# Branch A of an attention layer: transposed scores in blocks of 512 queries, row maxima from a product of their own, key tiles added on GpSimd

## What is computed

```python
s = jnp.einsum("btkgd,bskd->bkgts", q, k).astype(jnp.float32) * (q.shape[-1] ** -0.5)
p = jax.nn.softmax(s, axis=-1)
o = jnp.einsum("bkgts,bskd->btkgd", p.astype(v.dtype), v)
```

## Time and profile before

| | us |
|---|---|
| median of 3 runs | 5053.31 (5050.79 to 5055.74) |
| the profiled execution, its own time | 5050.44 |
| its span | 5048.9 |
| TensorE busy | 4546.0, 90% |
| VectorE busy | 3321.3, 66% |
| ScalarE busy | 2466.6, 49% |
| GpSimd busy | 1194.2, 24% |

### The profile page before, as it was taken

How to read it: one execution, slowest core, us unless ns; L and a number is a source line. 1 busy time by engine, 2 the same in 40 slices (tenths; PEclk the granted TensorE clock), 3 DMA queues, 4 the chain that set the end, 5 groups by cost and what they waited for, 6 DMA issues and landing times. The chain is left out here.

```text
span 5048.9 us, 75988 instructions
## 1 busy us (share of the span) xinstructions
PE 4546.0 (90%) x25973; PEld 3779.7 (75%) x25973; DVE 3321.3 (66%) x5284; ACT 2466.6 (49%) x3062; POOL 1194.2 (24%) x921
## 2 busy tenths in 40 slices
...
GB/s 186 204 120 146 63 77 80 96 177 144 206 198 174 192 214 261 397 397 397 397 359 176 190 99 147 63 88 98 124 193 209 120 163 166 384 397 397 397 397 334
DMA packets 580935, 1089.06 MB, mean 216 GB/s; under 512 B 111781, under 2 KB 265541, under 8 KB 577689
## 3 DMA queue, kind: packets, MB, share of 16 engines
...
## 5 line engine op out<-in xcount | busy, mean ns | idle before, releaser
L630 PE MATMUL project_proj_acc<-project_w_split,project_hT 128*128 128x512 f32 x2736 | 657.3, 397 | 4.1 <-DVE project_w_split L453 2.9
L1719 PE MATMUL merge_acc<-ahead_wide,merge_w_split 128*128 128x512 f32 (+1 forms) x2880 | 638.0, 376 | 21.8 <-DMA ahead_wide<-hT 14.4
L1719 PEld LDWEIGHTS merge_acc<-ahead_wide,merge_w_split 128*128 128x128 f32 x2880 | 504.9, 190 | 129.7 <-issue 21.5
L630 PEld LDWEIGHTS project_proj_acc<-project_w_split,project_hT 128*128 128x128 f32 x2736 | 511.5, 190 | 113.6 <-DVE project_hT L483 4.7
L2418 DVE TENSOR_TENSOR experts_w_gate<-experts_raw_gate,experts_w_gate 128x2048 fp32r<-128x2048 f32 x146 | 370.7, 2548 | 286.7 <-ACT experts_w_gate L2314 286.7
L2293 POOL TENSOR_TENSOR experts_w_down<-experts_raw_down,experts_w_down 128x2048 fp32r<-128x2048 f32 x73 | 354.4, 4855 | 512.1 <-ACT experts_w_down L2314 512.1
L947 DVE TENSOR_REDUCE attend_stat<-attend_scores 128x1 f32<-128x1280 f32 (+2 forms) x288 | 305.6, 1061 | 232.7 <-PE attend_scores L848 229.1
L2465 PE MATMUL experts_gate_acc<-experts_w_gate,experts_rowsT 128*128 128x512 f32 x1752 | 433.5, 403 | 12.3 <-DVE experts_rowsT L2423 6.5
L2479 PE MATMUL experts_result_acc<-experts_w_down,experts_hiddenT 128*128 128x512 f32 x1752 | 430.2, 401 | 12.2 <-DVE experts_w_down L2418 12.2
L2465 PE MATMUL experts_up_acc<-experts_w_up,experts_rowsT 128*128 128x512 f32 x1752 | 420.7, 396 | 0.0
L2465 PEld LDWEIGHTS experts_gate_acc<-experts_w_gate,experts_rowsT 128*128 128x128 f32 x1752 | 328.1, 191 | 99.5 <-issue 19.7
...
## 6 DMA issues: line engine op xcount, KB each, us to landing
...
experts_raw_up<-in_w_exp_up_dram SPq DMA_DIRECT2D x146, 1024.0 KB, 12.8
...
attend_keys<-qk SPq DMA_DIRECT2D x128, 320.0 KB, 5.8
...
```

Of the source, the lines that this page charges most:

```text
L630: m = pe.matmul(acc[g % 2][:, :], hT[:, a, q * KP + k, t * P:(t + 1) * P], w_split[:, n % SLOTS, c, k, :], start=(q == 0 and i == 0 and k ...
L1719: m = pe.matmul(acc[:, b, 0:w], w_split[b][:, a, k, :], hT[:, x, k, 0:w], start=(i == 0 and k == 0), stop=(i == 2 and k == KD - 1))
```

## The change

`attend_gqa` is split: branch C keeps it as `attend_c`, and branch A becomes `attend_a`, written out without a loop. Its unit is a span: one head and 512 latent queries (16 spans in a layer), or, in layer 0, the 256 context queries of both heads of a pair (4 spans more, third of the five of each pair). A span goes through its ten key tiles in five slots of two tiles (a context span has one slot).

- Keys are stationary and queries move, so that the scores come out transposed: for each key tile one product with 64 rows of high keys and a row of ones against the high queries and a row that holds the negative row maximum, and one product for the low parts; two matmuls of 512 columns for each key tile, four in a slot. The weights that the exponential writes need no transposes and no copies. The exponential (1024 wide, one in a slot) has no bias and sums nothing.
- The row maxima come from a product of their own, queries stationary and high keys moving: 8 products of 512 keys and 4 of 256 for a span, in ten pieces that each fill 512 columns of a PSUM bank; VectorE reduces each, and then the three numbers of each row to one. There are two such banks. An eleventh piece is the row itself: four matmuls turn the four columns of maxima into a negated row in PSUM, and ScalarE copies that row, one partition of 512, into the query tile. A plan made at build time (`SpanPlan`) puts the pieces of later spans between the slots; a span's row is due two slots ahead of its first slot.
- The row sums: GpSimd adds the weights of the ten key tiles (four additions of 1024 columns and one of 512 for a span), and TensorE sums over the partitions with one-column matmuls against ones, behind the four matmuls that turn the halves of the output. A context span has no additions: TensorE sums both tiles.
- The values are summed for the whole span behind its last slot: ten float32 products of 512 columns, alternating between the halves as before.
- ScalarE copies the halves (512 wide, once for a span), VectorE does one reciprocal and one multiplication of 256 elements.
- `qk` is loaded in other pieces: the high keys doubled, queries twice (both parts stacked; high parts alone), keys as three pieces.
- GpSimd runs A's additions first, then B's part, then the clearing, which now takes 80 DMAs of 128 rows of 1 KB instead of 20 of 4 KB. Branch C uses B's buffer of transposed weights, and its own probability buffers are 640 wide.

For layer 1 the plan puts these pieces in the slots of a span in the steady state: three, two, two, one and the row, two; the turn of the span before and the values stand behind the last.

```diff
--- before.py
+++ after.py
+class SpanPlan:
+    RATE, LEAD = 2.25, 2
+    def __init__(self, nq):
+        self.spans, slot = [], 0
+        for i in range(4):
+            order = [(0, 0), (0, 1), None, (1, 0), (1, 1)] if nq > NL else [(0, 0), (0, 1), (1, 0), (1, 1)]
+            for where in order:
+                if where is None:
+                    parts = [(hb, NL * P, 2 * P, hb * 2 * P) for hb in range(2)]
+                    tiles = list(range(NL, NT))
+                    pieces = [(2 * hb, 2, 0, [(hb, NL + t, NL * P, 2 * P, t * 2 * P) for t in range(2)])
+                              for hb in range(2)]
+                else:
+                    hb, half = where
+                    parts, tiles, pieces = [(hb, half * 512, 512, 0)], list(range(NT)), []
+                    for u in range(0, 4, 2):
+                        q = half * 4 + u
+                        pieces += [(u + t, 1, c, [(hb, q + t, c * 512, 512, 0)]) for t in range(2) for c in range(2)]
+                        pieces.append((u, 2, 2, [(hb, q + t, NL * P, 2 * P, t * 2 * P) for t in range(2)]))
+                self.spans.append(Span(len(self.spans), i, parts, tiles, slot, len(tiles) // 2, pieces))
+                slot += len(tiles) // 2
...
+        self.pieces = []
+        for s in self.spans:
+            for k, (j, count, c, products) in enumerate(s.pieces):
+                if s.n > 1 and k == min(3, len(s.pieces) - 1):
+                    self.add_row(s.n - 1)
+                self.pieces.append(Piece(s.n, len(self.pieces), j, count, c, products, False))
+            if s.n == 0:
+                self.add_row(0)
+        self.add_row(len(self.spans) - 1)
...
+        for s in self.spans:
+            k = max(s.first - self.LEAD, -1)
+            need[k] = max(need.get(k, 0), row_of[s.n] + 1)
...
+    def turn_slot(self, n):
+        if n + 1 == len(self.spans):
+            return len(self.slots)
+        if self.spans[n + 1].chunks > 1:
+            return self.last_slot(n + 1)
+        return self.spans[n + 2].first + 1
...
+def attend_a(nc, io, scr, l, nq, st, shared, rows):
...
+        def score(k):
+            s, c = plan.slots[k]
+            v = s.pair // 2
+            if c == 0:
+                pe.wait_ge(mw.sem, mw.done(s.n))
+                pe.wait_ge(k_in[v].sem, k_in[v].done(2))
+                for hb, _, _, _ in s.parts:
+                    pe.wait_ge(qh_in[hb].sem, qh_in[hb].done(s.pair))
+            if k >= 2:
+                pe.wait_ge(ex.sem, ex.done(k - 2))
+            for j in range(2):
+                kt = s.tiles[2 * c + j]
+                for hb, q0, w, col in s.parts:
+                    to = tops[k % 2][:, j * 512 + col:j * 512 + col + w]
+                    pe.matmul(to, keys[v][0:HD + 1, 0, kt * P:(kt + 1) * P], high[hb][0:HD + 1, q0:q0 + w],
+                              start=True, stop=False)
+                    m = pe.matmul(to, keys[v][:, 1, kt * P:(kt + 1) * P], both[hb][:, q0:q0 + w],
+                                  start=False, stop=True)
+            m.then_inc(sc.sem, 1)
+        def emit_piece(p):
+            v, to = spans[p.n].pair // 2, maxes[p.index % 2]
+            if p.index >= 2:
+                old = plan.pieces[p.index - 2]
+                if old.row:
+                    pe.wait_ge(mw.sem, mw.done(old.n))
+                else:
+                    pe.wait_ge(mp.sem, mp.done(plan.reduced[old.index]))
+            if p.row:
+                pe.wait_ge(mx.sem, mx.done(p.n))
+                for t in range(4):
+                    m = pe.matmul(to[:, t * P:(t + 1) * P], row_max[:, t, :], neg_ident[:, :], start=True, stop=True)
+                m.then_inc(mr.sem, 1)
+                return
+            for hb, qt, k0, w, col in p.products:
+                pe.wait_ge(q_in[hb].sem, q_in[hb].done(2 * spans[p.n].pair + 1))
+                m = pe.matmul(to[:, col:col + w], both[hb][:, qt * P:(qt + 1) * P], k_high[v][:, k0:k0 + w],
+                              start=True, stop=True)
+            m.then_inc(pm.sem, 1)
+        def turn_back(n):
+            b = n % 2
+            pe.wait_ge(hc.sem, hc.done(n))
+            if n in full:
+                pe.wait_ge(ps.sem, ps.done(full.index(n)))
+            for t in range(4):
+                pe.matmul(acc[b][:, t * HD:(t + 1) * HD], halves_out[b][:, t * P:(t + 1) * P], halves[:, :],
+                          start=True, stop=True)
+            parts = [sums[b]] if n in full else [ctxT[:, j, :] for j in range(2)]
+            for t in range(4):
+                for j, part_of in enumerate(parts):
+                    m = pe.matmul(acc[b][:, 4 * HD + t:4 * HD + t + 1], part_of[:, t * P:(t + 1) * P], ones[:, :],
+                                  start=(j == 0), stop=(j == len(parts) - 1))
+            m.then_inc(tb.sem, 1)
+        def sum_values(s):
+            b, v = s.n % 2, s.pair // 2
+            if s.n >= 2:
+                pe.wait_ge(yd.sem, yd.done(s.n - 2))
+            pe.wait_ge(v_in[v].sem, v_in[v].done(0))
+            for c in range(s.chunks):
+                pe.wait_ge(ex.sem, ex.done(s.first + c))
+                for j in range(2):
+                    m = pe.matmul(acc[b][j * HD:(j + 1) * HD, :], values[v][:, s.tiles[2 * c + j], :], weights_of(s, c)[:, j, :],
+                                  start=(c == 0), stop=(c == s.chunks - 1))
+            m.then_inc(pv.sem, 1)
+        pe.wait_ge(ready.sem, ready.done(0))
+        pe.wait_ge(km_in[0].sem, km_in[0].done(1))
+        for p in plan.pieces_of(-1):
+            emit_piece(p)
+        for k, (s, c) in enumerate(plan.slots):
+            score(k)
+            for p in plan.pieces_of(k):
+                if not p.row and spans[p.n].pair == 2:
+                    pe.wait_ge(km_in[1].sem, km_in[1].done(1))
+                emit_piece(p)
+            for n in range(s.n + 1):
+                if plan.turn_slot(n) == k:
+                    turn_back(n)
+            if c == s.chunks - 1:
+                sum_values(s)
+        turn_back(last)
+    def scalar(act):
+        def exps(k):
+            s, c = plan.slots[k]
+            old = plan.user_before(s.n, c)
+            act.wait_ge(sc.sem, sc.done(k))
+            if s.chunks == 1 and s.pair > 0:
+                act.wait_ge(tb.sem, tb.done(max(x.n for x in spans if x.chunks == 1 and x.n < s.n)))
+            elif s.chunks > 1 and old is not None:
+                act.wait_ge(pv.sem, pv.done(old))
+                act.wait_ge(pk.sem, pk.done(full.index(old) * 4 + max(c - 1, 0)))
+            act.activation(weights_of(s, c), tops[k % 2].rearrange("p (j n) -> p j n", j=2), ACT.Exp, scale=SCORE_SCALE
+                           ).then_inc(ex.sem, 1)
+        def write_row(p):
+            s = spans[p.n]
+            act.wait_ge(mr.sem, mr.done(p.n))
+            for n, (hb, q0, w, col) in enumerate(s.parts):
+                m = act.copy(high[hb][HD:HD + 1, q0:q0 + w], maxes[p.index % 2][HD:HD + 1, col:col + w])
+            m.then_inc(mw.sem, 1)
+        def copy_halves(n):
+            b = n % 2
+            act.wait_ge(pv.sem, pv.done(n))
+            if n >= 2:
+                act.wait_ge(tb.sem, tb.done(n - 2))
+            act.copy(halves_out[b][:, :], acc[b][:, :]).then_inc(hc.sem, 1)
...
+        def reduce_piece(p):
+            b = p.n % 2
+            x = plan.reduced[p.index]
+            dve.wait_ge(pm.sem, pm.done(x))
+            if p.j == 0 and p.c == 0 and p.n >= 2:
+                dve.wait_ge(mx.sem, mx.done(p.n - 2))
+            w = 512 // p.count
+            dve.tensor_reduce(part[:, b, p.j:p.j + p.count, p.c],
+                              maxes[p.index % 2].rearrange("p (t n) -> p t n", n=w), AX.X, ALU.max).then_inc(mp.sem, 1)
+            s = spans[p.n]
+            if (p.j, p.c) == (s.pieces[-1][0], s.pieces[-1][2]):
+                dve.wait_ge(mp.sem, mp.done(x))
+                if p.n >= 1:
+                    dve.wait_ge(mr.sem, mr.done(p.n - 1))
+                n_c = 3 if s.chunks > 1 else 1
+                dve.tensor_reduce(row_max[:, :, HD], part[:, b, :, 0:n_c], AX.X, ALU.max).then_inc(mx.sem, 1)
+        def finish(s):
+            b = s.n % 2
+            dve.wait_ge(tb.sem, tb.done(s.n))
+            dve.reciprocal(recip[:, b, :], acc[b][:, 4 * HD:4 * HD + 4]).then_inc(rc.sem, 1)
+            dve.wait_ge(rc.sem, rc.done(s.n))
+            for hb, q0, w, col in s.parts:
+                n, t0, c0 = w // P, q0 // P, col // P
+                if s.pair > 0:
+                    dve.wait_ge(y_out[hb].sem, y_out[hb].done(s.pair - 1))
+                m = dve.tensor_tensor(out[hb][:, t0:t0 + n, :],
+                                      acc[b][:, c0 * HD:(c0 + n) * HD].rearrange("p (t n) -> p t n", n=HD),
+                                      recip[:, b, c0:c0 + n].unsqueeze(2).to_broadcast([P, n, HD]), ALU.mult)
+            m.then_inc(yd.sem, 1)
...
+    def gpsimd(pool):
+        for f, n in enumerate(full):
+            s, two = spans[n], pooled[f % 2]
```

(19 more changed lines are left out.)

271 lines of the change are left out of this document (188 added, 83 removed).

## The result

The changed kernel takes 5067.3 us, the median of 7 runs (5061.8 to 5075.1), the kernel before 5052.4 us beside it (7 runs, 5046.9 to 5055.7). The ratio is 1.0034, with a 95% interval of 1.0022 to 1.0045: slower by 11 to 23 us, where 15 us less was forecast. The profiled execution has a span of 5062.7 us against 5048.9, so its 13.8 us more are what must be found.

A forecast was written before the change was run, and what follows sets the result against it. The prediction took TensorE, busy 90% of the span, as the bound. Layer 1's A -3.0, layer 0's -13.7 and the clock +1.5 made -15 us on 5050.44: 5035, given as 5036 for the median; range 5010 to 5070.

The forecast's parts named there:

- context span and the next, four: Layer 0's A: four context spans at 6.9 us each, 27.6 us instead of 38.3, each followed by a 15.25 us span.
- TensorE's work and its waits in a span: Steady span of A: 14.05 us of TensorE work plus 1.2 us of waits, 15.25 us against 15.48 for four old steps.
- VectorE's pace: Rival in A's spans: VectorE's reductions pace the slots, a span takes 16.35 us, +18, 5070 us; chance 0.20.
- by GpSimd's: Rival in A's spans: GpSimd's additions, at 2080 ns for 512, make a span 18.9 us, +94, 5145 us; chance 0.05.
- halves that don't run side by side: Rival in A's values products of 512 columns: 8.6 us of values, a span of 19.4 us, +109, 5160 us; chance 0.03.
- +1.5 for both layers (0 to 4): Start of A: TensorE works thinly during span 0's maxima, so its clock may rise later, costing 1.5 us in all.
- 8.5 + 15.25: Start of A in each layer: 8.5 us before the first scores (pieces 6.9, row 1.6), then span 0 at 15.25.
- 14 pieces instead of ten (+2): Span 0 of A: four more pieces in its slots cost 2 us, offset by having no turn (-2).
- Other waits 0.4: Layer 0's context spans: 0.4 us of the 6.9 each was allowed for waits besides that for their own exponential.
- 0.5 for GpSimd's last sum: End of A in each layer: 0.5 us waiting for GpSimd's last sum, within the 3.8 us until B starts.
- -7 to +4: Clearing in 80 issues beside branch C: its effect on the time lies between -7 and +4 us, taken as 0.
- p: A span's time in us: both layers' A take 79.3 + 30 p, forecast p 15.25, equal to the old 552.1 at 15.76.

The follow-up runs named there:

- the reduction test: The changed kernel with VectorE taking the maximum of only 32 columns of each group of a piece; 5037.6 us in one run.
- The dummies: The changed kernel plus 34 dummy TensorE products before A and two behind each of span 0's ten pieces; 5059.4 us, ratio 1.0024, starts 28.0 and 26.3 us.

## Why the prediction was wrong

Its sign was wrong, though the range up to 5070 holds the time. The sum for A, against the profiled execution:

| term | forecast | layer 0 | layer 1 |
|---|---|---|---|
| start, to the first copy of halves | 23.75 | 34.4 | 31.5 |
| full spans in the middle | 15.25 each | 10 of them, 151.3 | 14 of them, 217.3 |
| context span and the next, four | 22.15 each | 96.7 | |
| last span | 12.8 | 11.9 | 11.9 |
| till B | 3.8 | 6.8 | 7.1 |
| A | 281.5, 253.9 | 301.2 | 267.7 |

- **TensorE's work and its waits in a span** (14.05 and 1.2): right, 14.2 and 0.75 by the reduction test. Eleven of layer 1's fourteen middle spans are 0.25 us under the forecast, one 0.8; the other two are those of 19.5 and 18.3 us. The rivals by VectorE's pace, by GpSimd's and by halves that don't run side by side didn't occur.
- **The start** is the step that failed: "+1.5 for both layers (0 to 4)" for the clock, and 8.5 + 15.25. It is 10.7 and 7.7 us over, the largest of the misses. The dummies take 6.4 and 5.1 of it away, so the clock is 11.5 us in that pair of traces, where at most 4 were allowed. The direction had been named; the size wasn't worked out. The earlier trace rows had the row for it: the old A's first twelve matmuls, two steps' scores, take 4.60 us where the earlier trace rows has one step's in 1.27, and ten pieces, a row and a span with thin work had to be walked through at that rate.
- The remaining 4.3 and 2.6 us are the walk: span 0's slots carry the next span's pieces too, "14 pieces instead of ten (+2)", and no turn or values of an older span stand between them, so VectorE sets their pace. With dummies the first scores start 8.9 us after the first product (8.5), and the slots of span 0 take 14.5 and 12.9 us in place of the 10.8 of that step.
- **The context spans**: the first two, each with its successor, 23.0 us in place of 22.15; the other two 24.7 and 26.0, where the clock fell (the last pair takes 21.1 undisturbed): 8.1 us over in all. "Other waits 0.4" missed the 1.7 us wait for VectorE's result of two spans earlier: a short span brings that wait forward, which no long span has.
- **Till B**: "0.5 for GpSimd's last sum" was 3.0. In a steady span the sum is asked for 8.8 us after the values; the last span has no slots to hide it, and no pieces either, so its exponentials come faster than GpSimd adds. The turn then runs at half the clock. 3 us a layer.
- **The load order** wasn't costed at all. The query load of pair 1 is issued behind B's loads, and the first layer-1 span that needs it takes 19.5 us, a loss of 4.5; in the kernel with quick starts it is 15.5. What is queued ahead was asked for VectorE and the PSUM banks, not for SP.
- **The clearing**: -7 to +4, taken as 0; C of layer 0 gained 4.4 us by it alone and 7.9 with the change. Without it the result would be some 20 us slower: that the time still lies under 5070 is luck.
- **The rival that ended slower** was VectorE at every span, with p = 16.35. The time came out near its 5070 for another reason; p was 15.0 to 15.1.
- Two slips of the sums, neither of which matters: 5035 on the profiled execution and 2.9 more for the median make 5038, not 5036, and the three slower rivals add up to 0.28, not 0.25.

The Trainium skill (TensorE: Matmul & The Clock Gate, A second HAM failure mode) says that short idles between groups of matmuls, as banks of PSUM are cycled, can make the clock swing between its levels. The start here agrees in part. It has such gaps, 0.19 to 0.36 us between pieces, each ended by VectorE's read of a bank, and two longer ones of 1.08 and 0.67 us around the row; but the clock didn't swing there, it stayed at 0.50 for the two stretches shown.
